# A transformer block pair with an expert layer: gates in split format, lookup in PSUM, five edits at the turns between layers

## What is computed

```python
def adaln_norm(x, c, g, w_ada, b_ada):
    mod = jax.nn.silu(c) @ w_ada + b_ada
    shift, scale, gate = jnp.split(mod, 3, axis=-1)
    h = rms_norm(x, g) * (1.0 + scale[:, None, :]) + shift[:, None, :]
    return h, gate[:, None, :]
```

```python
def peer(h, wq, subkeys, u_tab, v_tab):
    q = (xt @ wq).reshape(T, PEER_HEADS, 2, PEER_HALF)
    sc = jnp.einsum('thpd,hpkd->thpk', q, subkeys).astype(jnp.float32)
    vals, ids = lax.top_k(sc, PEER_TOPK)                 # 16 of 128, per head and half
    cand = (vals[:, :, 0, :, None] + vals[:, :, 1, None, :]).reshape(T, PEER_HEADS, PEER_TOPK * PEER_TOPK)
    cid = (ids[:, :, 0, :, None] * PEER_KEYS + ids[:, :, 1, None, :]).reshape(...)
    top, pos = lax.top_k(cand, PEER_TOPK)                # 16 of 256, per head
    idx = jnp.take_along_axis(cid, pos, axis=-1)
    g = jax.nn.softmax(top, axis=-1)
    ...
        u = jnp.take(u_tab, ic, axis=0)                  # 128 experts of 16384 per token
        wgt = gc * jax.nn.gelu(jnp.einsum('chkd,cd->chk', u, xc))
        return jnp.einsum('chk,chkd->cd', wgt, jnp.take(v_tab, ic, axis=0))
```

## Time and profile before

| what | us |
|---|---|
| median of 3 runs | 2238.18 |
| the profiled execution, its time | 2242.05 |
| its span in the profile | 2240.2 |
| TensorE busy | 2175.6 (97%) |
| VectorE busy | 1571.8 (70%) |
| GpSimd busy | 1241.3 (55%) |
| ScalarE busy | 937.6 (42%) |

### The profile page before, as it was taken

How to read it: one execution, slowest core, us unless ns; L and a number is a source line. 1 busy time by engine, 2 the same in 40 slices (tenths; PEclk the granted TensorE clock), 3 DMA queues, 4 the chain that set the end, 5 groups by cost and what they waited for, 6 DMA issues and landing times.

```text
span 2240.2 us, 32178 instructions
## 1 busy us (share of the span) xinstructions
PE 2175.6 (97%) x11877; PEld 1944.6 (87%) x11877; DVE 1571.8 (70%) x3061; ACT 937.6 (42%) x1541; POOL 1241.3 (55%) x670
## 2 busy tenths in 40 slices
PE   6999999999999999999999999999999999999999
PEld 6897989888888877888999999999998888888887
DVE  5736777685556755552999999999974766666665
ACT  3235576432455414432434334555553333333332
POOL 1634222375223341242588788766657787778775
PEclk9999999999999999999999999999999999999999
DMA  7252424222221440232488788999989999999995
GB/s 281 88 186 106 144 92 133 73 104 95 95 85 57 147 154 20 76 133 103 148 269 287 266 291 267 344 357 328 352 301 345 368 348 357 351 348 361 356 359 217
DMA packets 164476, 492.42 MB, mean 220 GB/s; under 512 B 15072, under 2 KB 64608, under 8 KB 162912
## 3 DMA queue, kind: packets, MB, share of 16 engines
q1 hardware_dynamic: 107872, 305.79, 39.3%
q0 software_dynamic: 36864, 134.23, 16.1%
q10 hardware_dynamic: 19584, 50.34, 5.9%
HBM read 437.87 MB, written 52.43 MB: 219 GB/s over the span
## 4 chain that ended last, share of the span: by engine, by line
PE 40%; DVE 9%; POOL 2%; DMA 1%; issue 1%; ACT 0%; DVEq 0%; ACTq 0%; POOLq 0%
PE ps L2566 22%; PE ps L2530 14%; PE ps L2548 4%; POOL t_split L2675 1%; DVE arena L2794 1%; DVE arena L2763 1%; DVE arena L2754 1%; DVE arena L2755 1%; DVE rope L2732 1%; DVE arena L2759 1%; DVE norm_rows L2732 1%; DVE arena L2789 1%; DVE arena L2732 1%; DVE arena L2750 1%; DVE arena L2797 0%
## 5 line engine op out<-in xcount | busy, mean ns | idle before, releaser
L2675 POOL TENSOR_TENSOR t_split<-t_raw,t_split 128x1024 fp32r<-128x1024 f32 x225 | 550.1, 2446 | 220.1 <-ACT t_split L2601 218.1
L267 POOL TENSOR_TENSOR w_split<-ring,w_split 128x1024 fp32r<-128x1024 f32 x113 | 274.3, 2428 | 490.9 <-ACT w_split L259 445.0
L2530 PE MATMUL ps<-h_hi,t_split 128*128 128x384 f32 x2048 | 537.4, 338 | 7.4 <-POOL t_split L2675 4.4
L2566 PE MATMUL ps<-t_split,w_split 128*128 128x512 f32 x2304 | 522.8, 389 | 3.1 <-DVE t_split L2849 1.6
L2566 PEld LDWEIGHTS ps<-t_split,w_split 128*128 128x128 f32 x2304 | 432.3, 188 | 93.5 <-DVE t_split L2849 2.0
L2601 ACT ACTIVATE t_split<-t_raw 128x1024 fp32r<-128x1024 f32 x256 | 270.3, 1057 | 340.2 <-PE ps L2566 304.0
L291 PE MATMUL ps<-h_hi,w_split 128*128 128x512 f32 x1280 | 402.6, 392 | 0.0
L2530 PEld LDWEIGHTS ps<-h_hi,t_split 128*128 128x128 f32 x2048 | 373.4, 189 | 10.1 <-POOL t_split L2675 6.6
L2530 PE MATMUL ps<-h_lo,t_split 128*128 128x384 f32 x1024 | 343.9, 336 | 0.0
L291 PEld LDWEIGHTS ps<-h_hi,w_split 128*128 128x128 f32 x1280 | 240.3, 188 | 50.5 <-issue 0.7
L291 PE MATMUL ps<-h_lo,w_split 128*128 128x512 f32 x640 | 249.1, 389 | 0.0
(11 more groups left out here) (367 smaller groups left out, 3333.3 us busy)
## 6 DMA issues: line engine op xcount, KB each, us to landing
ring<-w_stream SPq DMA_DIRECT2D x203, 512.0 KB, 3.4
t_raw<-u_table SPq DMA_DIRECT2D x128, 512.0 KB, 4.8
t_raw<-v_table SPq DMA_DIRECT2D x128, 512.0 KB, 5.6
gelu_scratch<-e_gel ACTq DMA_DIRECT2D x128, 192.0 KB, 4.8
gates_scratch<-arena ACTq DMA_DIRECT2D x8, 3072.0 KB, 13.4
arena<-gelu_scratch SPq DMA_DIRECT2D x32, 768.0 KB, 5.9
arena<-gates_scratch SPq DMA_DIRECT2D x32, 768.0 KB, 8.8
first<-w_stream SPq DMA_DIRECT2D x16, 512.0 KB, 13.3
```

The costliest lines, as they stand in the source:

```text
L267: pool.tensor_tensor(w_split[:, i % RS, 1, :], ring[:, n % R, :], w_split[:, i % RS, 0, :].bitcast(F32), ALU.subtract).then_inc(lo_done, 1)
L2530: mm = pe.matmul(ps[:, 6 + n % 2, 0:NT], t_split[:, n % RAWS, u, k * P:(k + 1) * P], h_parts[h][:, k, P:T], start=(k + u + h == 0), stop=( ...
L2566: mm = pe.matmul(ps[:, 2 * i + half, :], w_split[:, b % 2, w, at:at + P], t_split[:, m % RAWS, v, half * 512:(half + 1) * 512], start=(n + ...
L2675: pool.tensor_tensor(t_split[:, m % RAWS, 1, :], t_raw[:, m % RAWS, :], t_split[:, m % RAWS, 0, :].bitcast(F32), ALU.subtract).then_inc(t_ ...
```

## The change

**Gates.** `hot_a` now holds, per token, two matrices in fp32r: the gate's upper part and its remainder at the first key. One three-operand instruction (comparison with a column as scalar, times a broadcast pair of columns) writes both. `hot_b` is fp32r too and is written by two instructions of 256 columns. TensorE makes two products of 128 columns per token. `selT` has a fourth row with the upper part, copied by ScalarE, and VectorE subtracts it once. `GATE_AT` is 68, and the selections stand behind tiles 35, 53 and 67.

**Lookup.** Two halves of 128x1024 in two banks of PSUM, with the sixteen numbers in PSUM as well.

**Turns.** The piece times the shifts is summed over the blocks by VectorE (`dve_share`, in the unit before the last of the projection) and TensorE needs one small product for it; the totals over units 0 to 6 are taken on TensorE inside the last unit, with half of the variance then done early (`dve_half`); the next layer's first products need only the upper part of block 0; two scaled blocks stand in PSUM; the query norm's steps come one unit later.

```diff
--- before.py
+++ after.py
@@ feature_unit
+                if pause and k == KD - 2:
+                    pause(pe)
...
@@ feature_group
-            if late:
-                for at in range(3):
+            if upper:
+                upper.wait(pe, 1)
+                for j in range(2):
+                    w[j] = piece_ready(pe, pieces[j])
+                    for a in range(2):
+                        pe.matmul(ps[:, banks[j], :], w[j][:, a, 0:P], src[0][:, 0, :], start=(a == 0), stop=False)
+                src_ready.wait(pe, 1)
+                for j in range(2):
+                    pe.matmul(ps[:, banks[j], :], w[j][:, 0, 0:P], src[1][:, 0, :], start=False, stop=False)
+                for at in range(1, 3):
...
@@ ColumnNorm.pe_opening
-                first = 3 - 2 * (self.sets - 1)
-                if self.sets == 2:
-                    self.pe_totals(pe)
-                products(range(first))
-                if self.sets == 1:
-                    self.pe_totals(pe)
+                before = 2 + self.sets
+                products(range(before - 1))
                 self.pe_last_sums(pe)
-                products(range(first, 6))
+                products(range(before - 1, 6 + (self.sets - 1) * 2))
                 self.inverted.wait(pe, 1)
                 self.pe_spread_set(pe, self.sets - 1)
-                products(range(6, KD)).then_inc(piece_used, 1)
-                for k in range(KD):
-                    mm = pe.matmul(ps[:, self.shift_bank, 0:1], ring[:, n % R, k * P:(k + 1) * P],
-                                   self.shifts[:, k:k + 1], start=(k == 0), stop=(k == KD - 1))
-                mm.then_inc(self.turned.sem, 1)
+                if self.sets == 1:
+                    products(range(6, KD))
+                self.share_summed.wait(pe, 1)
+                pe.matmul(ps[:, self.shift_bank, 0:1], share_sum, C("ones")[:, 0:1], start=True,
+                          stop=True).then_inc(self.turned.sem, 1)
...
@@ ColumnNorm, new
+            def dve_share(self, dve):
+                n = self.raw_unit
+                dve.wait_ge(piece_in[n % R], 16 * (n // R + 1 - FIRST_PIECES // R))
+                for k in range(KD):
+                    block = ring[:, n % R, k * P:(k + 1) * P]
+                    if k == 0:
+                        ins = dve.tensor_scalar(share_sum, block, self.shifts[:, 0:1], None, ALU.mult)
+                    else:
+                        ins = dve.scalar_tensor_tensor(out=share_sum, in0=block, scalar=self.shifts[:, k:k + 1],
+                                                       in1=share_sum, op0=ALU.mult, op1=ALU.add)
+                    if k < KD - 1:
+                        dve.wait_ge(dve_step, note("dve", ins))
+                ins.then_inc(self.share_summed.sem, 1)
+
+            def dve_half(self, dve):
+                self.half_summed.wait(dve, 1)
+                for s in range(self.sets):
+                    n = note("dve", dve.tensor_scalar(var[:, s * TT:(s + 1) * TT],
+                                                      ps[:, self.shift_bank, s * TT:(s + 1) * TT], 1.0 / D,
+                                                      EPS if s == 0 else 0.0, ALU.mult, ALU.add))
+                dve.wait_ge(dve_step, n)
...
+            def scaled_tile(self, k):
+                if self.raw_unit is not None and k in (2, 3):
+                    return ps[:, 7 if k == 2 else self.shift_bank, :]
+                return ntmp[:, k, :]
...
@@ out_projection
-                    feature_unit(pe, at + u, 4 + u % 3, h_parts)
+                    feature_unit(pe, at + u, 4 + u % 3, h_parts, pause=norm.pe_totals if u == KD - 1 else None)
...
-                    for v in {KD - 1: (KD - 3, KD - 2)}.get(u, (u - 2,) if u >= 2 else ()):
-                        norm.dve_raw(dve, v)
+                    if u >= 1:
+                        norm.dve_raw(dve, u - 1)
+                    if u == KD - 2:
+                        norm.dve_share(dve)
...
@@ query norm (the rope and the transposes of v move by one in the same way)
-                    for r in {6: (0, 1), 7: (2, 3), 8: (4,)}.get(u, ()):
+                    for r in {7: (0, 1), 8: (2, 3), 9: (4,)}.get(u, ()):
...
@@ experts
-        SEL_AT = {35: 1, 54: 2, 71: 3}
+        SEL_AT = {35: 1, 53: 2, 67: 3}
-        GATE_AT = 72
+        GATE_AT = 68
...
                     for s in range(QT):
-                        mm = pe.matmul(ps[:, q % NQ, s * P:(s + 1) * P], hot_b[:, q % NQ, s * P:(s + 1) * P],
-                                       hot_a[:, q % NQ * QT + s, :], start=True, stop=True)
+                        for part in range(2):
+                            mm = pe.matmul(ps[:, q % NQ, s * P:(s + 1) * P], hot_b[q % NQ * 2 + s // 2][:, s % 2, :],
+                                           hot_a[:, q % NQ * QT + s, part, :], start=(part == 0), stop=(part == 1))
...
+                    act.activation(selT[:, 3, tile_tokens(i)].bitcast(F32R), selT[:, 2, tile_tokens(i)],
+                                   ACT.Copy).then_inc(w_cut.sem, 1)
...
-                        step(dve.tensor_tensor(
-                            eq.rearrange("p h k a -> p (h k) a"),
-                            posab[:, j, :].unsqueeze(2).to_broadcast([P, P, PTOP]),
-                            C("iota16").unsqueeze(1).to_broadcast([P, P, PTOP]), ALU.is_equal))
-                        paced(2.3)
-                        step(dve.tensor_tensor(
-                            prod, eq, ids3[:, :, j, :].unsqueeze(2).to_broadcast([P, PH, PTOP, PTOP]), ALU.mult))
-                        paced(2.3)
-                        step(dve.tensor_reduce(sel[:, j, :], prod.rearrange("p h k a -> p (h k) a"), AX.X, ALU.add))
-                        paced(3.3)
+                        for half in range(2):
+                            of = slice(half * (P // 2), (half + 1) * (P // 2))
+                            heads = slice(half * (PH // 2), (half + 1) * (PH // 2))
+                            step(dve.tensor_tensor(
+                                match, posab[:, j, of].unsqueeze(2).to_broadcast([P, P // 2, PTOP]),
+                                iota_ps.unsqueeze(1).to_broadcast([P, P // 2, PTOP]), ALU.is_equal))
+                            paced(1.2)
+                            by_head = match.rearrange("p (h k) a -> p h k a", k=PTOP)
+                            step(dve.tensor_tensor(
+                                by_head, by_head, ids3[:, heads, j, :].unsqueeze(2).to_broadcast([P, PH // 2, PTOP, PTOP]),
+                                ALU.mult))
+                            paced(1.2)
+                            step(dve.tensor_reduce(sel[:, j, of], match, AX.X, ALU.add))
+                            paced(1.2)
...
+                        w_cut.wait(dve, TT - 1)
+                        step(dve.tensor_tensor(selT[:, 2, P:T], selT[:, 2, P:T], selT[:, 3, P:T], ALU.subtract))
...
-                    dve.tensor_tensor(hot_b[:, r, :].rearrange("p (t e) -> p t e", e=P),
-                                      ps[:, 3, 0:P].unsqueeze(1).to_broadcast([P, QT, P]),
-                                      selT[:, 1, t:t + QT].unsqueeze(2).to_broadcast([P, QT, P]),
-                                      ALU.is_equal).then_inc(hot, 1)
+                    for two in range(2):
+                        dve.tensor_tensor(hot_b[2 * r + two][:, :, :],
+                                          ps[:, 3, 0:P].unsqueeze(1).to_broadcast([P, 2, P]),
+                                          selT[:, 1, t + 2 * two:t + 2 * two + 2].unsqueeze(2).to_broadcast([P, 2, P]),
+                                          ALU.is_equal).then_inc(hot, 1)
...
-                        dve.tensor_scalar(hot_a[:, r * QT + s, :], ps[:, 3, 0:P], selT[:, 0, t + s:t + s + 1],
-                                          selT[:, 2, t + s:t + s + 1], ALU.is_equal, ALU.mult).then_inc(hot, 1)
+                        dve.scalar_tensor_tensor(out=hot_a[:, r * QT + s, :, :],
+                                                 in0=ps[:, 3, 0:P].unsqueeze(1).to_broadcast([P, 2, P]),
+                                                 scalar=selT[:, 0, t + s:t + s + 1],
+                                                 in1=selT[:, 2:4, t + s:t + s + 1].to_broadcast([P, 2, P]),
+                                                 op0=ALU.is_equal, op1=ALU.mult).then_inc(hot, 1)
```

107 lines of the change are left out of this document (58 added, 49 removed).

## The result

The changed kernel takes 2256.55 us (median of 11 runs, 2250.52 to 2261.53), the kernel before 2243.14 (median of 11, 2234.31 to 2251.62; the three runs shown ahead of the prediction were among them). The ratio is 1.0059, with a 95% interval from 1.0043 to 1.0076: slower by 13 us, where +3.4 was forecast. The range held it, but the size was off by a factor of four.

The account below looks back on a forecast made before the run. TensorE, busy 97%, bounds the kernel; VectorE was to become the bound of 48 gate tiles. Sweep +6.0, turns together −2.8 and constants' copy +0.2 made +3.4 us; 2241 us was said, range 2227 to 2262.

Parts of the forecast that it names:

- B: Gates: VectorE pays for a pointer and a broadcast operand, quad 2.486 us, sweep +29.5, total 2265 us; chance 0.13.
- C: Gates on TensorE: fp32r takes four passes at 128 columns, 7.57 us a tile, total 2307 us; chance 0.03.
- VectorE becomes the bound of the gates stage, quad 2.242 us: 48 gate tiles: VectorE needs 6.19 us a tile against TensorE's 5.95; a quad rises by 0.363 us.
- A: Gates: TensorE stays the bound, VectorE's quad costs only 2.00 us, total 2230 us; chance 0.13.
- Eight fp32r products cost what eight fp32 records cost: Gates on TensorE: 0.112 us each for a quad's eight, so TensorE gains nothing.
- D: Gates on TensorE: short weight loads, with VectorE's cheap form, sweep −17.0, total 2218 us; chance 0.05.
- Lookup −18.7 us, first matrix at 1363: Lookup on VectorE: 48 instructions at 1.25 us, 60.0 instead of 78.7 us; first hot matrix at about 1363.0.
- The sum of the sweep, +6.0: First sweep: 96 quads and 72 dots from the first matrix, then 12 tiles without gates; end 1711.0 instead of 1705.0.
- dots that wait for their rows: up to +15: First sweep held up elsewhere, by dots waiting for gathered rows, up to +15 us; chance 0.04.
- Turns 0, −0.5, 0: Turns between layers: gain 1.1 cancelled by a 1.1 us wait in first and third; second taken as −0.5 us.
- Query norm −2.3: Query norm: steps one unit later cover TensorE's 2.11 us wait, giving −2.3 us.
- The rule of the exclusive port: Share in the turns: if its first two-operand instruction precedes GpSimd's split, GpSimd is held; a turn gives −1.1 us, not 0.

Follow-up runs that it names:

- one_part_rows7: `rows7` with only the upper part's product of the gates on TensorE, the lower part left out of the sum; one execution, sweep 639.5 us.
- rows7: The changed kernel with all seven gathered-row buffers in turn from dot 51 instead of 60, opened at 284 us planned instead of 300; ratio to before 1.0008.
- experts_only: The kernel before with the expert layer's edits alone (gates, four tiles sooner, lookup), turns as before; ratio 1.0061.
- before_rows7: The kernel before with the seven row buffers in turn from dot 53 on; one execution, 2228.03 us.
- turns_only: The kernel before with the edits at the turns alone, expert layer as before; ratio 1.0000 (0.9981 to 1.0019).

## Why the prediction was right or wrong

The range held the result by luck: 2256.55 lies 15.6 us above the 2241 that was said, in a part of the range that stood open for the rivals B and C, and neither came true. By the prediction's own line (above 2249.4) it lies on the slower side, which had a chance of 0.22.

- **VectorE becomes the bound of the gates stage, quad 2.242 us:** right (2.23; a tile 6.17, between the 5.95 and 6.4 that would have refuted it; busy 220.00 of 220.00; `one_part_rows7`). A and B fell with it: neither 2.00 nor 2.49. The row of L719 carried over to another operation, width and operand.
- **Eight fp32r products cost what eight fp32 records cost:** right (5.96 us between groups against 5.95). C and D fell. The fast load that the Trainium skill, "TensorE: Matmul & The Clock Gate", section "Weight-path perf modes — Fast Weight Load (FWL) and DoubleRow", gives to 128 weights of a type other than FP32 did not show for fp32r (0.11 us a product); the earlier trace rows were the better guide.
- **Lookup −18.7 us, first matrix at 1363:** the 48 instructions take 1.22 to 1.23 us each; timeline of the changed kernel:

```profile
1344.29 1.22 DVE L2838 TENSOR_TENSOR ps<-arena,ps 128x1024 f32<-128x1024 f32 x1
1345.55 1.23 DVE L2843 TENSOR_TENSOR ps<-ps,arena 128x1024 f32<-128x1024 f32 x1
1346.81 1.22 DVE L2847 TENSOR_REDUCE arena<-ps 128x64 f32<-128x1024 f32 x1
```

  1.26 apart where 1.25 was taken. The first matrix came at 1357.7, 290.8 us into the sweep; forecast were 292.7 (1363.0 less the sweep's start at 1070.35).
- **The sum of the sweep, +6.0: this step failed.** "From there 96 quads × 2.242 and 72 dots × 1.137, together 297.1" has every piece right and leaves out a term of +12.1 us: dots that wait for their rows. I asked of VectorE's new speed only what it costs, not what it overtakes. The rows are issued by GpSimd at table tiles fixed at build time, three buffers deep until dot 60, and I moved VectorE 23 us against those tiles (first hot matrix 290.8 us into the sweep, 313.9 in the earlier trace rows). With the term taken away by `rows7` the sweep is 640.1, +3.8 on 636.3, near the forecast of +6.0. In the prediction this case stood as "dots that wait for their rows: up to +15" with a chance of 0.04; that chance, and no place in the sum, was the error.
- **Turns 0, −0.5, 0:** the collision was right in place and size (xT of unit 6 late by 2.4, forecast 2.7; wait 0.6, forecast 1.1; net 0 to 0.1 us in the first and the third turn). The second was wrong in sign, though its wait was less than forecast (1.83, not 2.7): against executions without the fall of the clock it costs 3.5 us, against the one with it 0.7. Rows 13 were one execution's: with the old turns the granted clock fell in one of three, and with the wait of 1.83 us (2.54 with the share in unit 2) that the change puts there it is 0.79 to 0.89 over 16 us in all eleven executions of kernels with the changed turns. Windows of `experts_only` and of the changed kernel, each from the same place in the turn:

```profile
728.14:744.14 16.00, 15.92 (x102) 14.02 (x101) 9.79 (x28) 7.52 (x13) 6.46 (x3) 1.00 0.04 8
```
```profile
732.89:748.89 16.00, 15.52 (x85) 13.08 (x84) 7.00 (x25) 5.69 (x10) 4.74 (x2) 0.89 0.21 68
```

- **Query norm −2.3:** its wait is gone, and the stretch with it and the third turn is 4 to 6 us shorter at the median. The rest goes with the granted clock: each of the three executions with the old steps has it at the lower level once or twice more between the second turn and the third, 3.4 us each time (0.50 over 908.7 to 912.1 in the kernel before; 0.51 over 784.1 to 787.5, right behind a wait of 2.43 us for L2058, and 0.50 over 907.0 to 910.4 in `experts_only`; 0.51 over 782.0 to 785.4 in `before_rows7`), and nine of the eleven with the new steps do not. At half the clock each of these costs some 1.7 us, an estimate from its length. Together the turns came to about −1 to −4, forecast −2.8, and `turns_only` says 0 ± 4: within the bounds, but by luck: the second turn's loss cancels what the query norm gives beyond its forecast.
- **The rule of the exclusive port** (the Trainium skill, "SBUF — State Buffer", section "Who interferes with whom"), as weighed in the prediction, would have given −1.1 a turn had the share come first. Its first instruction with two SBUF operands came 0.05 us after GpSimd's split (430.09 and 430.04) and was held, as forecast; the trace agrees with the rule (4.82 us instead of 2.68).

## What to carry to other kernels

When an edit makes an engine faster or lets it start sooner, list what that engine consumes and who issues it on what schedule; the wait that appears there can be larger than the time saved, and it costs nothing in a profile taken before. A price taken from the nearest row with the same number of pointers and operands, less its elements, was good to 1% here, even across operations. And read a turn's cost from stretches between common instructions in several executions: a single profile against another gave 7 us where the timing gives none.
